# One tile of squares for the norms of a four layer network, and their sum one step later

## Chip, cores and metric
The kernel runs on one core of a Trainium2 chip. The metric is the device time of one execution in microseconds, as the median of several runs. TensorE multiplies, ScalarE applies functions and casts, VectorE and GpSimd do elementwise work, SyncE issues the DMAs.

## What is computed
Two layers of one block, then two of another, on 256 tokens of 1024 features in float32. Every layer normalises its input twice. Cut to what matters here:

```python
def rms_norm(x, w):
    y = x * lax.rsqrt(jnp.mean(x * x, axis=-1, keepdims=True) + 1e-6) * w
for l in range(2):                       # layers 0 and 1
    h = rms_norm(x, mix_pre_norm[l]);  m = hybrid_mixer(h, w_in[l], ...)
    x = x + rms_norm(m, mix_post_norm[l])
    h = rms_norm(x, ffn_pre_norm[l])
    x = x + rms_norm((silu(h @ w_gate) * (h @ w_up)) @ w_down, ffn_post_norm[l])
for l in range(2):                       # layers 2 and 3
    h = h + hybrid_mixer_2(rmsnorm(h, attn_norm[l]), w_in[l], ...)
    h = h + square(relu(rmsnorm(h, mlp_norm[l]) @ w_up[l])) @ w_down[l]
return rmsnorm(h, final_norm)
```
The eight norms ahead of a projection are those of the change. The first projection of a mixer is `qkv` (with a convolution of four taps along time and a Silu behind it), of an attention `q2a`, of an ffn `gu`, of an mlp `up`.

## The kernel before
Activations are kept turned: features on the 128 partitions, 256 tokens along the row, eight tiles `xT`. Weights stream in blocks of 128 x 1024 (`raw`, four slots), block after block over the whole network. ScalarE casts each to its high half (`whi`), VectorE, for some blocks (`SHARED`) GpSimd, subtracts it to get the low half (`wlo`, four slots). A product of float32 is three products: high weights with high and low activations, low weights with high activations; a block has 24 of them. In the mixers' `qkv` blocks 4, 8 and 12 of the layer are GpSimd's.

A norm is taken after the projection. The input is only scaled by its gain and split (`hh`, `hl`), the projection runs on that, and a factor per token, `RSB` = exp(-0.5 ln(mean + eps)), is multiplied in when a pair of result tiles is read out of its bank. The sum over features is made with a matrix of ones: ScalarE squares four pairs of tiles (`SQ2`, 128 x 512 each), GpSimd adds pair 0 to pair 1 and pair 2 to pair 3 (`squares`), TensorE multiplies the four halves with ones into one bank (`norm_sum`), ScalarE takes Ln and Exp (`factor`), VectorE turns the factor for the norms in `BY_TOKEN`.

Every engine runs its own queue in the order of the program. Each walks a projection in steps (`Job.steps`): step 0 has blocks 0 and 1, then one block a step; every second step completes a pair of tiles, which is read out (`evac`: VectorE multiplies by `RSB`; in `qkv` ScalarE then makes the first tap and VectorE three more for each tile). At each step ScalarE and VectorE first split the blocks of `STAGED`, which are two to four blocks ahead: at step 0 blocks 2 and 3, at step 1 blocks 4 and 5. The `hook` is the norm's part: on TensorE `norm_sum` behind step 0, on ScalarE and VectorE the factor behind the splits of step 0, ahead of the first pair. In a mixer, `next(qkv)` twice, then the small products of the gates (`SW`, 16 and 8 columns), then `delta(L)`, whose first part is a chain of tiny instructions with Exp and Ln between VectorE and ScalarE. ScalarE holds one table of functions at a time; Exp and Ln share one, Silu has another.

Of the kernel before, what the change touches and what calls it, by code (L numbers as in the profile page):

```python
# [15 lines left out]
T = 256  # L16
# [248 lines left out]
def program(nc, ins, out):  # L265
    with ExitStack() as ctx:
# [338 lines left out]
        def scalar(a):  # L605
# [20 lines left out]
            def project(name, L, evac=None, hook=None):  # L626
                for chunks, done in JOBS[name, L].steps():
# [3 lines left out]
                    if hook and len(chunks) == 2:  # L631
                        hook()
                    for m0 in done:
                        if evac:
                            a.wait_ge(*proj.at(name, L, m0))
                            evac(m0)
# [189 lines left out]
            def first(L):  # L826
# [30 lines left out]
                next(qkv)  # L857
                a.wait_ge(*v_dn.at("ab", L))
# [195 lines left out]
        def vector(v):  # L1054
# [14 lines left out]
            def project(name, L, evac=None, hook=None):  # L1069
                for chunks, done in JOBS[name, L].steps():  # L1070
# [3 lines left out]
                    if hook and len(chunks) == 2:  # L1074
                        hook()
                    for m0 in done:
                        if evac:
                            evac(m0)
# [236 lines left out]
            def first(L):  # L1315
# [20 lines left out]
                qkv = project("qkv", L, conv, hook)  # L1336
                next(qkv)
# [315 lines left out]
        def gpsimd(g):  # L1653
# [18 lines left out]
            def squares(norm, j):  # L1672
                if j % 2:
                    g.wait_ge(*a_norm.at("square", norm, j))
                    tt(pair(SQ2, j), pair(SQ2, j), pair(SQ2, j - 1), OP.add).then_inc(*g_norm.up("squares", norm, j))

            def all_squares(then):
                for j in range(4):
                    squares(then, j)
# [88 lines left out]
            def first(L):  # L1768
                qkv = project("qkv", L)
                next(qkv)  # L1770
                next(qkv)
                dn = delta(L)
# [68 lines left out]
            for j in range(4):  # L1841
                squares("mixpre0", j)
# [9 lines left out]
        def tensor(e):  # L1852
# [30 lines left out]
            def project(name, L, xh, xl, ready, hook=None, after=None):  # L1883
                job = JOBS[name, L]
                for chunks, done in job.steps():
                    if len(chunks) == 2:
# [11 lines left out]
                        if hook:  # L1898
                            hook()
                    else:  # L1900
                        i = chunks[0]
                        e.wait_ge(*wlo_at(i))
                        for q in range(8):
# [11 lines left out]
                            elif full:  # L1915
                                x.then_inc(*proj.up(*full))
                    if after:
# [97 lines left out]
            def norm_sum(norm):  # L2015
# [3 lines left out]
                for j in (1, 3):  # L2019
                    e.wait_ge(*g_norm.at("squares", norm, j))  # L2020
                    for k in range(2):
                        x = mm(bank[b][:, 0:T], C("ones"), pair(SQ2, j)[:, k * T:(k + 1) * T], (j, k) == (1, 0), (j, k) == (3, 1))
                x.then_inc(*e_norm.up("sum", norm))
# [194 lines left out]
            def first(L):  # L2218
                norm = f"mixpre{L}"
                h = hh, hl, stream_ready(norm)  # L2220
                qkv = project("qkv", L, *h, lambda: norm_sum(norm))
                next(qkv)
# [352 lines left out]
```

## Time and profile before

| | |
|---|---|
| median of 3 runs | 1928.36 us (1928.3 to 1932.68) |
| profiled execution, its own time | 1935.99 us |
| its span | 1934.2 us |
| TensorE busy | 1887.0 us, 98% |
| VectorE busy | 1238.2 us, 64% |
| ScalarE busy | 958.4 us, 50% |
| GpSimd busy | 311.4 us, 16% |
| chain that ended last | PE 83%, DVE 12%, ACT 4% |

The profile names the engines PE (TensorE), DVE (VectorE), ACT (ScalarE), POOL (GpSimd) and SP (SyncE). A row of the timeline has the start and the length in us, the engine, the line, the operation, what is written and read with their shapes, how many in a row, and in brackets the idle time of the engine before it with what ended it. A float32 product with ones is two rows' worth, so four of them are x8. Products overlap their neighbours: the distance of two starts is what one costs.

### The profile page before, as it was taken

The numbers are of one execution on the slowest core, as the hardware profiler recorded it, in microseconds if no ns is written. First come the engines' busy times: TensorE is split into PE (matmuls) and PEld (weight loads), VectorE is DVE, ScalarE is ACT, GpSimd is POOL, SyncE is SP. The second block draws the span as 40 slices with busy tenths as digits, with TensorE's granted clock in tenths as the row PEclk, the third lists the DMA queues.
The fourth block names the chain that finished last, engine by engine and source line by source line (L and its number), as shares of the span: only waits on it lengthen the run. The fifth ranks groups of instructions, "written<-read, shape, count | busy, mean of one in ns | idle before, by whom it ended". The sixth has DMA issues, their size and how long they took to land.

```text
span 1934.2 us, 35101 instructions
## 1 busy us (share of the span) xinstructions
PE 1887.0 (98%) x14820; PEld 1800.6 (93%) x14820; DVE 1238.2 (64%) x1667; ACT 958.4 (50%) x1375; POOL 311.4 (16%) x174
## 2 busy tenths in 40 slices
PE   7999999999999999999999999999999999999998
PEld 7989998998889999999988999999999999999997
DVE  6884577665579545867657775577646684567743
ACT  5533365544563344654445445655534444656632
POOL 1050121000014102200001352310000353220000
PEclk9999999999999999999999999999999999999999
DMA  5443344656344323545665553345555763345652
GB/s 209 158 138 108 121 161 140 215 196 205 134 142 159 115 99 127 201 164 186 196 206 176 178 190 121 132 153 198 188 186 172 219 191 123 131 161 176 197 196 99
DMA packets 91580, 317.50 MB, mean 164 GB/s; under 512 B 11552, under 2 KB 12704, under 8 KB 91040
## 3 DMA queue, kind: packets, MB, share of 16 engines
q1 hardware_dynamic: 91424, 315.26, 48.7%
q8 instruction: 118, 1.93, 0.4%
q14 instruction: 38, 0.31, 0.0%
HBM read 304.99 MB, written 1.05 MB: 158 GB/s over the span
## 4 chain that ended last, share of the span: by engine, by line
PE 83%; DVE 12%; ACT 4%; issue 1%; DMA 0%; SPq 0%; ACTq 0%; DVEq 0%
PE bank L1863 81%; DVE wlo L1056 4%; DVE area L1056 3%; DVE area L1062 2%; ACT area L618 1%; ACT whi L624 1%; PE bank L2302 1%; PE bank L2042 1%; DVE xT L1062 0%; DMA raw<-in_weights 0%; DVE hl L1062 0%; DVE area L1527 0%; ACT hh L618 0%; DVE area L1525 0%; PE bank L2320 0%
## 5 line engine op out<-in xcount | busy, mean ns | idle before, releaser
L1056 DVE TENSOR_TENSOR wlo<-raw,whi 128x1024 fp32r<-128x1024 f32 x512 | 657.0, 1296 | 427.6 <-ACT whi L624 427.2
L1863 PE MATMUL bank<-hh,whi 128*128 128x256 f32 x2928 | 834.0, 285 | 26.4 <-DVE wlo L1056 18.7
L1863 PE MATMUL bank<-hl,whi 128*128 128x256 f32 x2928 | 817.6, 279 | 0.0
L1863 PE MATMUL bank<-hh,wlo 128*128 128x256 f32 x2928 | 817.4, 279 | 0.0
L624 ACT CAST whi<-raw 128x1024 fp32r<-128x1024 f32 x572 | 588.2, 1046 | 398.5 <-PE bank L1863 368.5
L1863 PEld LDWEIGHTS bank<-hh,whi 128*128 128x128 f32 x2928 | 556.9, 190 | 41.8 <-issue 15.1
L1863 PEld LDWEIGHTS bank<-hl,whi 128*128 128x128 f32 x2928 | 556.0, 190 | 1.5 <-issue 1.4
L1863 PEld LDWEIGHTS bank<-hh,wlo 128*128 128x128 f32 x2928 | 555.7, 190 | 0.0
L1655 POOL TENSOR_TENSOR area<-area 128x512 f32<-128x512 f32 (+4 forms) x90 | 138.3, 1544 | 929.8 <-ACT area L618 675.9
L1655 POOL TENSOR_TENSOR wlo<-raw,whi 128x1024 fp32r<-128x1024 f32 x60 | 151.5, 2526 | 332.1 <-ACT whi L624 331.7
L1863 PE MATMUL bank<-area 128*128 128x128 f32 (+5 forms) x1544 | 200.3, 289 | 4.1 <-DVE area L1056 3.3
L1863 PEld LDWEIGHTS bank<-area 128*128 128x128 f32 (+2 forms) x1544 | 181.2, 188 | 18.4 <-DVE area L1056 4.6
L1863 PE MATMUL bank<-FH,whi 128*128 128x256 f32 x640 | 178.6, 279 | 0.0
L1863 PE MATMUL bank<-FL,whi 128*128 128x256 f32 x640 | 178.3, 279 | 0.0
L1863 PE MATMUL bank<-FH,wlo 128*128 128x256 f32 x640 | 178.2, 279 | 0.0
L618 ACT ACTIVATE area<-area 128x256 f32<-128x256 f32 (+9 forms) x247 | 140.0, 578 | 60.3 <-DVE area L1056 20.7
L1056 DVE TENSOR_TENSOR area<-bank,area 128x512 f32<-128x512 f32 (+4 forms) x194 | 116.6, 629 | 57.1 <-PE bank L1863 52.9
L1863 PEld LDWEIGHTS bank<-FH,whi 128*128 128x128 f32 x640 | 121.5, 190 | 0.1
L1863 PEld LDWEIGHTS bank<-FL,whi 128*128 128x128 f32 x640 | 120.1, 188 | 0.1
L1863 PEld LDWEIGHTS bank<-FH,wlo 128*128 128x128 f32 x640 | 120.1, 188 | 0.0
L1056 DVE TENSOR_TENSOR area<-bank,RSB 128x512 f32<-128x512 f32 (+1 forms) x118 | 80.4, 682 | 51.4 <-PE bank L1863 51.4
L1863 PE MATMUL bank<-wlo,FH 128*128 128x512 f32 x240 | 94.6, 394 | 0.0
(123 smaller groups left out, 1883.6 us busy)
## 6 DMA issues: line engine op xcount, KB each, us to landing
raw<-in_weights SPq DMA_DIRECT2D x572, 512.0 KB, 3.7
area<-area SPq DMA_DIRECT2D x96, 64.0 KB, 3.7
area<-area SPq DMA_DIRECT2D x16, 128.0 KB, 3.8
cst<-in_const SPq DMA_DIRECT2D x1, 1188.0 KB, 10.1
cst<-in_const SPq DMA_DIRECT2D x1, 1024.5 KB, 5.6
xT<-in_x SPq DMA_DIRECT2D x4, 256.0 KB, 5.8
out<-xT SPq DMA_DIRECT2D x1, 1024.0 KB, 3.8
area<-in_lev SPq DMA_DIRECT2D x2, 384.0 KB, 7.7
```

What stands on the lines that cost most here:

```text
L618: return a.activation(dst, src, fn, scale=scale, **more)
L624: a.copy(whi[:, i % RING, :], raw[:, i % RAW, :]).then_inc(*hi.up(i))
L1056: return v.tensor_tensor(dst, x, y, op)
L1062: return v.scalar_tensor_tensor(out=dst, in0=x, scalar=s, in1=y, op0=op0, op1=op1)
L1655: return g.tensor_tensor(dst, x, y, op)
L1863: return e.matmul(ps, x, y, start=start, stop=stop, skip_group_check=skip)
L2042: x = e.transpose(bank[b0 + j][:, 128 * (b % 4):128 * (b % 4) + 128], block(src, b), C("eye"))
L2302: o = e.transpose(bank[b][:, 128 * u:128 * u + 128], x.grid()[:, j % 2, j // 2, 128 * kb:128 * kb + 128], C("eye"))
```

## The change
GpSimd adds the squares up further: the two sums of pairs to one, and its two halves to one tile of 128 x 256. TensorE multiplies that one tile with ones. The hook stands behind step 1 in place of step 0, on all three engines, and the first pair of tiles is read out behind it. In the mixers the part behind the second `next(qkv)` now stands behind a third. VectorE's `project` is changed as ScalarE's, and its, GpSimd's and TensorE's `next(qkv)` too.

```diff
@@ ScalarE
             def project(name, L, evac=None, hook=None):
-                for chunks, done in JOBS[name, L].steps():
+                first_pair = []
+                for step, (chunks, done) in enumerate(JOBS[name, L].steps()):
                     for i in chunks:
                         for s in STAGED[i]:
                             split(s)
-                    if hook and len(chunks) == 2:
+                    if hook and step == 0:
+                        first_pair, done = done, []
+                    if hook and step == 1:
                         hook()
+                        done = first_pair + done
                     for m0 in done:
...
                 qkv = project("qkv", L, conv, hook)
+                next(qkv)
                 next(qkv)
                 next(qkv)
...
@@ GpSimd
-            def squares(norm, j):
-                if j % 2:
-                    g.wait_ge(*a_norm.at("square", norm, j))
-                    tt(pair(SQ2, j), pair(SQ2, j), pair(SQ2, j - 1), OP.add).then_inc(*g_norm.up("squares", norm, j))
-
             def all_squares(then):
-                for j in range(4):
-                    squares(then, j)
+
+                for j in (1, 3):
+                    g.wait_ge(*a_norm.at("square", then, j))
+                    tt(pair(SQ2, j), pair(SQ2, j), pair(SQ2, j - 1), OP.add).then_inc(*g_norm.up())
+                g.wait_ge(*g_norm.now())
+                tt(pair(SQ2, 3), pair(SQ2, 3), pair(SQ2, 1), OP.add).then_inc(*g_norm.up())
+                g.wait_ge(*g_norm.now())
+                tt(SQ2[:, 1536:1536 + T], SQ2[:, 1536:1536 + T], SQ2[:, 1536 + T:2048], OP.add).then_inc(*g_norm.up("squares", then))
...
@@ TensorE
-                        if hook:
-                            hook()
                     else:
...
+                    if hook and step == 1:
+                        hook()
                     if after:
...
                 fresh(b, a_norm.at("log", norm))
-                for j in (1, 3):
-                    e.wait_ge(*g_norm.at("squares", norm, j))
-                    for k in range(2):
-                        x = mm(bank[b][:, 0:T], C("ones"), pair(SQ2, j)[:, k * T:(k + 1) * T], (j, k) == (1, 0), (j, k) == (3, 1))
-                x.then_inc(*e_norm.up("sum", norm))
+                e.wait_ge(*g_norm.at("squares", norm))
+                mm(bank[b][:, 0:T], C("ones"), SQ2[:, 1536:1536 + T], True, True).then_inc(*e_norm.up("sum", norm))
```

TensorE, start of layer 0 (block 1's last products, the ones, block 2; `bank0` is the norm's). Before:

```order
L1863 MATMUL bank4<-hl_58,whi_51 128x256
L1863 MATMUL bank4<-hh_57,wlo_52 128x256
L1863 MATMUL bank0<-area_61,cst_53 128x256 [waits norm_pool]
L1863 MATMUL bank0<-area_61,cst_53 128x256
L1863 MATMUL bank0<-area_61,cst_53 128x256 [waits norm_pool]
L1863 MATMUL bank0<-area_61,cst_53 128x256
L1863 MATMUL bank5<-hh_57,whi_51 128x256 [waits wlo_dve]
L1863 MATMUL bank5<-hl_58,whi_51 128x256
L1863 MATMUL bank5<-hh_57,wlo_52 128x256
```

Now:

```order
L1874 MATMUL bank4<-hl_58,whi_51 128x256
L1874 MATMUL bank4<-hh_57,wlo_52 128x256
L1874 MATMUL bank5<-hh_57,whi_51 128x256 [waits wlo_dve]
L1874 MATMUL bank5<-hl_58,whi_51 128x256
...
L1874 MATMUL bank5<-hl_58,whi_51 128x256
L1874 MATMUL bank5<-hh_57,wlo_52 128x256
L1874 MATMUL bank0<-area_61,cst_53 128x256 [waits norm_pool]
L1874 MATMUL bank5<-hh_57,whi_51 128x256 [waits wlo_dve]
L1874 MATMUL bank5<-hl_58,whi_51 128x256
```

The four products with ones stood between blocks 1 and 2; one stands between blocks 2 and 3.

ScalarE, first projection of layer 0, from the factor on (`RSB` from `bank0` is its Ln, `CAST whi` a high half, 128x8 the gates' chain, 128x512 a Silu and the squares behind it). Before:

```order
L618 ACTIVATE RSB_59<-bank0,cst_53 128x256 [waits norm_pe]
...
L624 CAST whi_51<-raw_50 128x1024 [waits proj,raw0]
L624 CAST whi_51<-raw_50 128x1024 [waits proj,raw1]
L618 ACTIVATE area_61<-area_61 128x8 [waits delta_dve] x2
L618 ACTIVATE area_61<-area_61,cst_53 128x8 [waits delta_act]
L618 ACTIVATE area_61<-par_54 128x8
L624 CAST whi_51<-raw_50 128x1024 [waits proj,raw2]
L618 ACTIVATE area_61<-area_61,par_54 128x256 [waits evac_dve,proj]
L618 ACTIVATE area_61<-area_61,par_54 128x256
L618 ACT_TABLE_LOAD
```

Now, from the two high halves that stand ahead of the factor:

```order
L624 CAST whi_51<-raw_50 128x1024 [waits proj,raw0]
L624 CAST whi_51<-raw_50 128x1024 [waits proj,raw1]
L618 ACTIVATE RSB_59<-bank0,cst_53 128x256 [waits norm_pe]
...
L624 CAST whi_51<-raw_50 128x1024 [waits proj,raw2]
L618 ACTIVATE area_61<-area_61,par_54 128x256 [waits evac_dve,proj]
L618 ACTIVATE area_61<-area_61,par_54 128x256
L618 ACT_TABLE_LOAD
L618 ACTIVATE area_61<-area_61 128x512 [waits delta_dve]
L618 ACTIVATE area_61<-area_61 128x512 [waits delta_act]
L611 ACT_TABLE_LOAD [waits delta_dve]
L618 ACTIVATE area_61<-area_61 128x8
L618 ACTIVATE area_61<-area_61 128x8 [waits delta_dve]
```

The high halves of blocks 4 and 5 have moved ahead of the factor, the second pair's tap and the first pair's Silu ahead of the gates' chain, and two table loads have come in, one ahead of that chain's first Exp and one, below these rows, ahead of the next Silu.

GpSimd, start of layer 0 (`area` 128x512 and 128x256 are the squares, `wlo` are low halves of blocks 4, 8 and 12). Before:

```order
L1655 TENSOR_TENSOR area_61<-area_61 128x512 [waits norm_act] x2
L1655 TENSOR_TENSOR wlo_52<-raw_50,whi_51 128x1024 [waits whi,ldhead]
L1655 TENSOR_TENSOR wlo_52<-raw_50,whi_51 128x1024 [waits whi] x2
L1655 TENSOR_TENSOR area_61<-area_61 128x1024 [waits delta_dve,delta_pe,ldc1]
L1709 COPY area_61<-area_61 128x1024 [waits evac_dve]
```

Now:

```order
L1665 TENSOR_TENSOR area_61<-area_61 128x512 [waits norm_act] x2
L1665 TENSOR_TENSOR area_61<-area_61 128x512 [waits norm_pool]
L1665 TENSOR_TENSOR area_61<-area_61 128x256 [waits norm_pool]
L1665 TENSOR_TENSOR wlo_52<-raw_50,whi_51 128x1024 [waits whi,ldhead]
L1665 TENSOR_TENSOR wlo_52<-raw_50,whi_51 128x1024 [waits whi] x2
```

Two adds stand between the squares and the low half of block 4, each behind a wait for the one before.

## Rows read from the trace of the kernel before

**Rows 1.** Page, costliest groups, TensorE (busy, mean ns; idle before, releaser):
```profile
L1863 PE MATMUL bank<-hh,whi 128*128 128x256 f32 x2928 | 834.0, 285 | 26.4 <-DVE wlo L1056 18.7
```

**Rows 2.** Timeline, TensorE, mixer 0 (start, length, what, times; idle before):
```profile
19.22 1.89 PE L1863 MATMUL bank<-area,cst 128*128 128x256 f32 x8
21.06 0.28 PE L1863 MATMUL bank<-hl,whi 128*128 128x256 f32 x1
```

**Rows 3.** Timeline, TensorE, attention 2, the key's norm:
```profile
1059.18 0.59 PE L1863 MATMUL bank<-area,cst 128*128 128x256 f32 x2
```

**Rows 4.** Timeline, GpSimd, TensorE and VectorE, ffn of layer 0:
```profile
332.83 2.53 POOL L1655 TENSOR_TENSOR area<-area 128x512 f32<-128x512 f32 x2 [30.89 <-ACT area L618]
...
334.46 2.09 PE L1863 MATMUL bank<-area,cst 128*128 128x256 f32 x8
...
334.77 1.68 DVE L1056 TENSOR_TENSOR wlo<-raw,whi 128x1024 fp32r<-128x1024 f32 x1 [2.15 <-ACT whi L624]
...
336.51 0.38 PE L1863 MATMUL bank<-hh,whi 128*128 128x256 f32 x1
...
339.33 0.28 PE L1863 MATMUL bank<-hh,whi 128*128 128x256 f32 x1
...
342.29 0.38 PE L1863 MATMUL bank<-hh,whi 128*128 128x256 f32 x1
```

**Rows 5.** Timeline, mixer of layer 1, then attention of layer 2:
```profile
521.66 2.53 POOL L1655 TENSOR_TENSOR area<-area 128x512 f32<-128x512 f32 x2 [186.30 <-ACT area L618]
...
525.33 0.38 PE L1863 MATMUL bank<-hh,whi 128*128 128x256 f32 x1
...
1032.91 1.60 DVE L1056 TENSOR_TENSOR wlo<-raw,whi 128x1024 fp32r<-128x1024 f32 x1 [2.21 <-ACT whi L624]
...
1034.57 0.38 PE L1863 MATMUL bank<-hh,whi 128*128 128x256 f32 x1
```

**Rows 6.** Timeline, VectorE and TensorE, mlp of layer 2:
```profile
1297.98 1.72 DVE L1056 TENSOR_TENSOR wlo<-raw,whi 128x1024 fp32r<-128x1024 f32 x1 [0.52 <-ACT whi L624]
...
1299.74 1.89 PE L1863 MATMUL bank<-area,cst 128*128 128x256 f32 x8
...
1307.58 0.38 PE L1863 MATMUL bank<-hh,whi 128*128 128x256 f32 x1 [0.50 <-DVE wlo L1056]
```

**Rows 7.** Timeline, GpSimd and VectorE where they meet, mixer 0:
```profile
25.81 2.35 POOL L1655 TENSOR_TENSOR wlo<-raw,whi 128x1024 fp32r<-128x1024 f32 x1 [10.76 <-ACT whi L624]
...
121.12 2.39 POOL L1655 TENSOR_TENSOR area<-area 128x1024 f32<-128x1024 f32 x1
...
121.39 3.20 DVE L1056 TENSOR_TENSOR wlo<-raw,whi 128x1024 fp32r<-128x1024 f32 x1 [1.67 <-ACT whi L624]
...
123.46 2.29 POOL L1655 TENSOR_TENSOR area<-area 128x512 f32<-128x512 f32 x1
```

**Rows 8.** Timeline, VectorE, mixer 0, first projection:
```profile
22.10 0.43 DVE L1056 TENSOR_TENSOR area<-RSB,cst 128x256 f32<-128x256 f32 x1 [4.83 <-ACT RSB L618]
24.36 5.12 DVE L1062 SCALAR_TENSOR_TENSOR area<-area,par 128x255 f32<-128x255 f32 x6 [0.64 <-ACT area L618]
...
33.97 1.23 DVE L1056 TENSOR_TENSOR wlo<-raw,whi 128x1024 fp32r<-128x1024 f32 x1 [0.67 <-ACT whi L624]
36.43 2.96 DVE L1062 SCALAR_TENSOR_TENSOR area<-area,par 128x255 f32<-128x255 f32 x6 [0.64 <-ACT area L618]
40.39 1.22 DVE L1056 TENSOR_TENSOR wlo<-raw,whi 128x1024 fp32r<-128x1024 f32 x1 [0.99 <-ACT whi L624]
```

**Rows 9.** Timeline, ScalarE, same stretch:
```profile
36.82 1.28 ACT L618 ACT_TABLE_LOAD   x1
38.11 1.30 ACT L618 ACTIVATE area<-area 128x512 f32<-128x512 f32 x2
```

**Rows 10.** Timeline, TensorE, later in mixers 0 and 1:
```profile
54.28 0.39 PE L1863 MATMUL bank<-hh,whi 128*128 128x256 f32 x1 [0.73 <-DVE wlo L1056]
...
545.86 0.39 PE L1863 MATMUL bank<-hh,whi 128*128 128x256 f32 x1 [1.43 <-DVE wlo L1056]
```

More of the change, by code:

```diff
@@ L1069, in project @@
             def project(name, L, evac=None, hook=None):
-                for chunks, done in JOBS[name, L].steps():
+                first_pair = []
+                for step, (chunks, done) in enumerate(JOBS[name, L].steps()):
                     for i in chunks:
@@ L1073, in project @@
                             split(s)
-                    if hook and len(chunks) == 2:
+                    if hook and step == 0:
+                        first_pair, done = done, []
+                    if hook and step == 1:
                         hook()
+                        done = first_pair + done
                     for m0 in done:
@@ L1336, in first @@
                 qkv = project("qkv", L, conv, hook)
+                next(qkv)
                 next(qkv)
@@ L1771, in first @@
                 next(qkv)
+                next(qkv)
                 dn = delta(L)
@@ L1839, in second @@
                     all_squares("attn3")
-            for j in range(4):
-                squares("mixpre0", j)
+            all_squares("mixpre0")
             g.wait_ge(s_head, 16)
@@ L1884, in project @@
                 job = JOBS[name, L]
-                for chunks, done in job.steps():
+                for step, (chunks, done) in enumerate(job.steps()):
                     if len(chunks) == 2:
@@ L1916, in project @@
                                 x.then_inc(*proj.up(*full))
+                    if hook and step == 1:
+                        hook()
                     if after:
@@ L2221, in first @@
                 qkv = project("qkv", L, *h, lambda: norm_sum(norm))
+                next(qkv)
                 next(qkv)
```

## The prediction

> **What bounds the kernel now.** I read the page's groups first: TensorE is busy almost all the time, and its idle time in front of the first product of a weight block is 26.4 us over 2928 products, of which 18.7 us end with a low half (wlo) from VectorE [rows 1]. So a microsecond of products taken away shortens the run only where the next block's low half is ready; elsewhere it turns into idle time. I therefore went to each of the eight places with the timeline, all engines side by side, and asked there what releases the first product of the third weight block. I call the blocks of a projection 0, 1, 2, ... and their low halves wlo(0), wlo(1), ...
>
> **What the sum costs TensorE.** In layer 0 the four products with ones are eight passes; from their start to the second product of block 2 it is 21.06 - 19.22 = 1.84 us [rows 2]. A product of 256 columns takes (339.33 - 336.51) / 24 = 0.12 us [rows 4], so the four cost 1.72 us, 0.43 each. The one kind of place with a single such product agrees: its two passes take 0.59 us where the eight take 1.89 [rows 2, 3], and (1.89 - 0.59) / 3 is 0.43. Three removed at eight places are at most 8 x 1.29 = 10.3 us. That is the ceiling of this part, and 0.53% of the time.
>
> **Where that is hidden already.** In the ffn of layer 0 step 0 ends at 334.46, the sum fills 334.46 to 336.51, and block 2 starts at 336.51. But wlo(2) ran from 334.77 for 1.68 us, so until 336.45; block 2 starts 0.06 us after it [rows 4]. TensorE could not have begun block 2 earlier. The sum lies in a wait that is there anyway. With the change TensorE idles from 334.58 to 336.5, starts block 2 at the same time, and then pays for the one product, 0.43, plus about 0.15 for the restart after waits. Before, block 4 began at 342.29, 0.13 later than two blocks of 2.83 after 336.51 would give; that bit goes. The place becomes 0.45 slower (the sum of ffn 1 shows the same times from its start). The attention of layer 2 is alike: wlo(2) ends at 1034.51, block 2 starts at 1034.57 [rows 5]. Its block 4 had no such bit to lose, so it gets 0.6 slower. In the mixer of layer 1 the squares end at 524.19 and block 2 starts at 525.33 [rows 5], in the same order of events; its account is below.
>
> At the two mlp and in the attention of layer 3 the squares come earlier. In the first mlp wlo(2) ends at 1299.70, when step 0 does, at 1299.74 [rows 6]. Block 2 can follow at once, three products (1.29) are saved, and the wait of 0.50 for wlo(4) in front of block 4 [rows 6] goes too, because ScalarE now splits blocks 4 and 5 ahead of its wait for the sum. Less a restart and a short wait for GpSimd (0.3): -1.5 at each mlp, -1.1 in the attention of layer 3, which has no such wait.
>
> **The two new adds on GpSimd.** Two adds of 512 columns take 2.53 us together [rows 4], so the third takes 1.27 and the one of 256 columns, by half, 0.64. They meet VectorE. A VectorE instruction of two SBUF operands doesn't run beside one of GpSimd: a low half that started at 121.39 inside a GpSimd instruction that ended at 123.51 took 3.20 us instead of 1.22, and GpSimd's next one, begun at 123.46, took 2.29 instead of 1.27: it stood until VectorE was done at 124.59 [rows 7]. The two take turns. So the third add waits for wlo(2) and runs to 337.6, wlo(3) then ends at 338.7, the fourth add at 339.3. TensorE wants the sum at 339.33. It fits with nothing to spare, hence the 0.1 to 0.2 us per place above; if VectorE won the turn once more it would be 1.1 us at each of seven places.
>
> **The mixers' first projection.** Here VectorE is the bound: TensorE waits 0.73 for it at 54.28 in layer 0, and 1.43 at 545.86 in layer 1 [rows 10]. So it is VectorE's chain from the factor on that counts, up to wlo(7), at 40.39 in layer 0 [rows 8]. Step by step, layer 0:
> factor: the sum starts 2.83 us later (a block) and is three products shorter (1.29): +1.54;
> the six taps of the first pair took 5.12 us, those of the second 2.96, because GpSimd's wlo(4), at 25.81 for 2.35, stood against them [rows 7, 8]; wlo(4) is now made ahead of the factor, in VectorE's idle time: -2.16;
> wlo(5) too, which stood in the chain: -1.2 (its 1.22, overlapped by 0.08);
> the third step now lies ahead of the gates' small chain and holds the second pair, with its Silu. The small chain needs Exp and Ln again. The order above shows three table loads where there was one; the load takes 1.28 [rows 9]. The one ahead of the first Exp lies in VectorE's path: +1.28. The second Silu load sits beside the taps of the third pair: +0.2;
> VectorE's waits for high halves (0.67 ahead of 33.97, 0.99 ahead of 40.39 [rows 8]) become one of 0.7: -1.0.
> Sum -1.3 us for layer 0.
> The Trainium skill (ScalarE: Activation LUTs, "What ACT_TABLE_LOAD costs") puts a switch of tables at about 2.7 us with its drain. The trace differs: the load at 36.82 takes 1.28, and the function behind it starts at 38.11, with no drain to be seen [rows 9]. By the page's figure the loads would cost 2.8 us more over both layers and the sum would turn to +1.4 us.
>
> Layer 1 differs in one thing: the first two adds end only at 524.19 [rows 5], so the four fill GpSimd to about 528.2, and wlo(4) is done behind them and behind VectorE's wlo(5), from 529.2 to 531.5. The factor's product on VectorE is due at 529.8 and has two SBUF operands: it stands until 531.5. The chain starts 5.1 us late instead of 1.5. Sum +2.4 us. Without that collision it is +0.8; and TensorE idles for about 1 us ahead of the gates' products and 3.5 us ahead of block 7.
>
> **Other queues.** SyncE waits for low halves only, and those of blocks 4 and 5 come earlier. The swaps of the rope wait for products that come 1 to 3 us later; the fetch behind the first of them waits for wlo(6), which stands behind that product on VectorE anyway: nothing. The factor reads the norm's bank at once after the sum, and a projection wants that bank back two blocks later at the earliest: no wait.
>
> **Sum.** -1.3 (mixer 0) + 2.4 (mixer 1) + 0.9 (two ffn) + 0.6 (attention 2) - 3.0 (two mlp) - 1.1 (attention 3) = -1.5 us. The profiled execution took 1935.99 us, its span 1934.2; the median of the runs is 1928.36. I take the difference over as it is: 1934.5 for a profiled execution, 1927 for the median.
>
> **Rivals.**
> 1. The products were the cost, as a count of TensorE's work would have it: the low halves come earlier too, because ScalarE and VectorE no longer stand at the factor. Then the 10.3 us come, and the waits of 0.5 at the two mlp: 1918. Against it: wlo(2) depends on nothing that the change moves, and it gates four of the eight places. A half-way form, mixers gaining 2.5 each, gives 1922. Together 0.13; about 0.11 of it beyond 0.3%.
> 2. Slower: the place is VectorE's chain in the mixers' projection. Its order against GpSimd shifts, and the two later halves that GpSimd makes in each layer, wlo(8) and wlo(12), fall wholly on taps, as wlo(4) did at 2.16. That is a bound, since a part of it is paid now: four times 2.16 is 8.6 us, and the sum ends at 1935.6. It decides from 7.3 us lost in both layers together, which is the 0.3% and my gain of 1.5. For it: the shift of 1.5 and 5.1 us is certain, and a tap that meets a half has always waited for the whole of it. Against it: VectorE's chain sets when both are made, so they move together. Chance 0.14.
> 3. GpSimd wins the ports ahead of wlo(2), or VectorE wins them once more ahead of the fourth add: 1.1 to 1.3 us (one add, or one low half) at seven places, 1935. Against it the row of 123.46 [rows 7], and the semaphore between the adds. Chance 0.08.
> 4. The change moves what it says, but later waits for VectorE swallow or return it: within 2 us of 1928. This is part of the forecast's range.
> 5. A table load costs more in the path than its 1.28 us, at most twice that: two in each layer make 2.6 to 5.1 us, 1930 to 1932. Against it the row of 38.11 [rows 9]. Chance 0.03, inside the forecast's range; this is what the page's figure would do.
>
> **How the numbers follow.** Forecast 0.65, its own range 1923 to 1932; rival 1 0.13, 2 and 3 0.22. About 0.3% (5.8 us) is what a measurement of this kernel tells from no change. Faster than that: 0.13 (rival 1 and a tail of the forecast). Slower: 0.18 (most of 2 and 3). Same: 0.69. The range 1921 to 1935.5 holds the forecast, the half-way form of rival 1 and the near half of 2 and 3.
>
> **What the new profile would show.** In both ffn and in attention 2: idle TensorE of about 1.9 us ahead of block 2, ended by a low half, block 2 at the same distance from step 0 as before. In both mlp: no wait ahead of block 2, none ahead of block 4. On ScalarE three table loads in each mixer's first projection. In layer 1 a factor's product of about 2 us on VectorE, under a GpSimd instruction, and a wait of TensorE of about 3 us ahead of block 7. The prediction is wrong if wlo(2) starts earlier than now, if the third add delays it, or if the waits in the mixers differ from this by more than 2 us.

## The result, and the profile after

The changed kernel took 1941.15 us (median of 11 runs, 1935.41 to 1950.37), the kernel before 1932.68 (11 runs, 1926.9 to 1938.17): ratio 1.0046, 95% interval 1.003 to 1.0061. It is slower, and the forecast of 1927.0 with 0.69 on "same" was wrong. The forecast started from the 1928.36 of three runs of the kernel before; from the 1932.68 of eleven its -1.5 us would be 1931.2, and the measured difference is +8.5. The profiled execution of the changed kernel took 1940.96 us, 4.97 more than that of before.

Page of the changed kernel, TensorE's first group, the one of [rows 1]:

```profile
L1874 PE MATMUL bank<-hh,whi 128*128 128x256 f32 x2928 | 840.3, 287 | 32.2 <-DVE wlo L1061 24.5
```

The idle time ahead of these products rose by 5.8 us, all of it ended by low halves. But the mean product also became 2 ns longer (287, before 285), though the array does the same. The forecast had no term for that. I laid the 12,720 products with high and low halves of both traces side by side, one by one, and read how far the second is behind at the start of each block. "So far" adds up:

| place | forecast | measured | so far |
|---|---|---|---|
| mixer 0 | -1.3 | -1.3 | -1.3 |
| between, clock | | +1.6 | +0.3 |
| ffn 0, up to block 4 | +0.45 | +1.9 | +2.3 |
| ffn 0, the rest of `gu` | 0 | +4.1 | +6.4 |
| mixer 1 | +2.4 | +2.2 | +8.6 |
| between, clock | | -1.5 | +7.1 |
| ffn 1, up to block 4 | +0.45 | +2.0 | +9.1 |
| ffn 1, the rest of `gu` | 0 | +3.1 | +12.2 |
| attention 2 | +0.6 | +2.1 to +2.4 | +14.6 |
| between, pace and clock | | +0.6 | +15.2 |
| mlp 2, up to block 4 | -1.5 | -1.4 | +13.8 |
| mlp 2, the rest of `up`, and `down` | 0 | -6.4 | +7.4 |
| attention 3 | -1.1 | -0.9 | +6.5 |
| between | | +0.2 | +6.7 |
| mlp 3 | -1.5 | -1.7 | +5.0 |

Timeline of the changed kernel, in order of time: ScalarE in mixer 0; ffn 0, from its block 0 on; GpSimd and VectorE in mixer 1; the sum of mlp 2.

```profile
31.65 1.28 ACT L618 ACT_TABLE_LOAD   x1
...
34.75 1.28 ACT L611 ACT_TABLE_LOAD   x1 [0.51 <-DVE area L1061]
...
41.70 1.28 ACT L618 ACT_TABLE_LOAD   x1
...
328.89 0.35 PE L1874 MATMUL bank<-hh,whi 128*128 128x256 f32 x1 [1.58 <-DVE hl L1067]
...
333.17 6.44 POOL L1665 TENSOR_TENSOR area<-area 128x512 f32<-128x512 f32 x4 [30.87 <-ACT area L618]
...
335.11 6.72 DVE L1061 TENSOR_TENSOR wlo<-raw,whi 128x1024 fp32r<-128x1024 f32 x4 [2.14 <-ACT whi L624]
...
336.84 0.38 PE L1874 MATMUL bank<-hh,whi 128*128 128x256 f32 x1 [1.88 <-DVE wlo L1061]
...
338.00 0.42 PE L1874 MATMUL bank<-hh,wlo 128*128 128x256 f32 x1
...
341.29 0.59 PE L1874 MATMUL bank<-area,cst 128*128 128x256 f32 x2
...
528.07 6.43 POOL L1665 TENSOR_TENSOR area<-area 128x512 f32<-128x512 f32 x4 [188.46 <-ACT area L618]
534.47 3.37 POOL L1665 TENSOR_TENSOR wlo<-raw,whi 128x1024 fp32r<-128x1024 f32 x1
...
537.79 0.43 DVE L1061 TENSOR_TENSOR area<-RSB,cst 128x256 f32<-128x256 f32 x1 [2.20 <-ACT RSB L618]
...
1318.10 0.67 PE L1874 MATMUL bank<-area,cst 128*128 128x256 f32 x2
```

In ffn 0 the order of events is the forecast one, up to block 2: TensorE idles 1.88 us and starts when the low half is there, and the four adds end at 339.61 (forecast 339.3). But where [rows 4] have 2.83 us for a block, block 2 now takes 341.29 - 336.84 = 4.45: its products last 0.42 from 337.7 on. TensorE by stretch says why (length, busy time with the number of products, then PEclk, the granted clock: 1.00 is 2.4 GHz, 0.50 is 1.2 GHz; then the DMA's share and GB/s). The changed kernel:

```profile
334.80:336.80 2.00, 0.17 (x2) 1.00 0.00 0
337.70:341.10 3.40, 3.40 (x18) 0.50 0.74 242
342.00:345.00 3.00, 3.00 (x27) 1.00 0.81 264
849.70:853.10 3.40, 3.40 (x18) 0.50 0.62 193
1047.70:1051.00 3.30, 3.30 (x18) 0.50 0.75 223
...
345.00:449.00 104.00, 104.00 (x885) 1.00 0.59 193
...
1320.00:1465.00 145.00, 145.00 (x1282) 1.00 0.62 200
```

The three rows at 0.50 stand right behind the idle time of ffn 0, ffn 1 and attention 2. Each costs about 1.6 us, and the trace of before has none in these places. This is the first missing term.

The second: behind block 4 the clock is full again, and still the changed kernel falls back, evenly, by 0.1 us a block. The last two rows show it as a number of products, in `gu` of layer 0 and from `up` of layer 2 into the `down` that follows it without a wait. The same two stretches of the kernel before, run a second time:

```profile
345.00:449.00 104.00, 104.00 (x920) 1.00 0.62 205
...
1320.00:1465.00 145.00, 145.00 (x1233) 1.00 0.58 187
```

In 104 us at full clock TensorE starts 885 products in the one and 920 in the other: 117.5 and 113.0 ns each. In `up` it is the other way round. By the distances of single starts there are two values only in these stretches, 113.3 and 117.8 ns, and a stretch keeps its value until TensorE waits or runs a product of another kind (a foreign product, such as the one with ones). I call them the fast and the slow pace, and name a stretch by the projection that it starts in. The Trainium skill (TensorE: Matmul & The Clock Gate, "Wait — 56ns, not 53.3ns?") gives a product at full clock its columns by 2.4 GHz and 2.5 ns more, for 256 columns an estimate of 109 ns; the trace has neither that nor a single value.

At the mlp the forecast held: block 2 and block 4 wait no more than 0.04 us, where [rows 6] had 0.50, and the one product stands behind block 2. ScalarE's table loads in mixer 0 stand where the order had them, 1.28 us each as in [rows 9]. In mixer 1 the size was right (+2.2) and the way was not: the factor's product on VectorE was to stand under GpSimd's low half for about 2 us. It takes 0.43, because half clock at 532 had made the sum so late that GpSimd was done, at 537.84. Nor is there a wait of 3 us ahead of block 7.

### The profile page after: what moved, and what is told of

Same layout as the page of the kernel before. It is cut to its first block, busy times and chain, and to the rows that moved or that the text cites. A ratio compares the mean times of both kernels' runs of the same rounds, so it can differ in the third digit from the quotient of the medians.

```text
span 1939.2 us, 35025 instructions
## 1 busy us (share of the span) xinstructions
PE 1886.2 (97%) x14772; PEld 1802.5 (93%) x14772; DVE 1247.7 (64%) x1667; ACT 964.0 (50%) x1379; POOL 338.7 (17%) x190
## 4 chain that ended last, share of the span: by engine, by line
PE 85%; DVE 10%; ACT 4%; issue 1%; DMA 0%; SPq 0%; DVEq 0%; ACTq 0%
PE bank L1874 83%; DVE wlo L1061 4%; DVE area L1061 3%; ACT area L618 2%; ACT whi L624 1%; DVE area L1067 1%; PE bank L2311 1%; DVE xT L1067 1%; PE bank L2050 1%; ACT hh L618 0%; DVE hl L1067 0%; DMA raw<-in_weights 0%; PE bank L2329 0%; DVE area L1119 0%; ACT L618 0%
## 5 line engine op out<-in xcount | busy, mean ns | idle before, releaser
L1061 DVE TENSOR_TENSOR wlo<-raw,whi 128x1024 fp32r<-128x1024 f32 x512 | 665.9, 1315 | 427.0 <-ACT whi L624 426.5
L1874 PEld LDWEIGHTS bank<-hh,wlo 128*128 128x128 f32 x2928 | 561.9, 192 | 0.0
L1665 POOL TENSOR_TENSOR area<-area 128x512 f32<-128x512 f32 (+4 forms) x106 | 165.7, 1570 | 919.8 <-ACT area L618 666.8
L1874 PE MATMUL bank<-whi,FL 128*128 128x512 f32 x240 | 94.4, 393 | 0.0
```

Source lines behind the costliest of these rows:

```text
L1061: return v.tensor_tensor(dst, x, y, op)
L1665: return g.tensor_tensor(dst, x, y, op)
L1874: return e.matmul(ps, x, y, start=start, stop=stop, skip_group_check=skip)
```

## The experiments

Two theories went into the first runs. A: what TensorE idles at four places costs more than the time it idles, by the clock and the pace behind it. B: VectorE's chain in the mixers' first projections costs it (my rival 2). The first expectation alone calls something else theory B: that the pace comes out by chance in each execution.

**The kernel before, again**, to see what a trace varies by itself.

> The kernel before, unchanged, as a control: how much of the difference between two executions is not the change. Theory A (the extra time of the change comes from what the idle time at the four places does to TensorE's clock): ratio 1.000, and no half-clock window behind the first products of an ffn, an mlp or an attention, as in the first profile. Theory B (the pace of the products, 113 or 118 ns, is chance from execution to execution, and the two profiles differ by such luck): the profile shows the slow pace in other stretches than the first one (there: layer 2's mlp, 1308 to 1480 us), and its length can differ by up to 6 us.

Measured: 1933.26 against 1932.36 us, ratio 1.0002 [0.999, 1.0015]. No half clock stands at the places of the ffn, mlp and attentions, and the slow pace is in `up` of layer 2 again, as in the first trace.

**The tile alone, the hook in its old place.**

```diff
@@ the kernel before
-                for j in (1, 3):
-                    e.wait_ge(*g_norm.at("squares", norm, j))
-                    ... four products
+                ... and the four adds on GpSimd, as in the change
+                e.wait_ge(*g_norm.at("squares", norm))
+                mm(bank[b][:, 0:T], C("ones"), SQ2[:, 1536:1536 + T], True, True).then_inc(*e_norm.up("sum", norm))
```

> Only the first part of the change: the squares added up to one tile, one product with ones, at the old place behind step 0. By my account of GpSimd's adds (the third waits for wlo(2), the fourth for wlo(3)) TensorE waits for the tile: at ffn 0 the tile is there at 339.3 where step 0 ends at 334.5, so 3.2 us slower than before at each of the two ffn, the attention of layer 2 and the mixer of layer 1 there hidden in part; about 1.8 slower at each mlp and attention 3; mixer 0 1.3 faster. Sum +12 us, ratio 1.006, more if the waits lower the clock (1.009). If the adds are not held up by VectorE (rival), the tile is there 2.0 us after the pairs and the sum is +4 us, ratio 1.002.

Measured: 1960.45 us, ratio 1.0147 [1.0116, 1.0178]. TensorE stands in front of the one product until GpSimd's adds end:

```profile
338.06 1.19 PE L1863 MATMUL bank<-area,cst 128*128 128x256 f32 x2 [4.75 <-POOL area L1655]
```

Four places idle 4.7 us, as the expectation's times give for ffn 0 (339.3 less 334.5), and three more 2.7 to 2.9; each of the first four has half clock at the end of its idle time or right behind it, and so have two of the three. The loss is above the expected 1.006 to 1.009; in the trace 11.9 of its 25.2 us are half clock (table below), and the rest is near the expected 12. Here the adds themselves are late; the step's delay is what hides them.

**The step alone, four products and two adds as before.**

```diff
@@ the changed kernel
-                mm(bank[b][:, 0:T], C("ones"), SQ2[:, 1536:1536 + T], True, True).then_inc(*e_norm.up("sum", norm))
+                for j in (1, 3):
+                    ... the four products and their waits, and GpSimd's two adds
```

> Only the second part: the hook one step later, the first pair behind it, a third step ahead of the gates in the mixers; the squares stay two tiles of 512 columns and TensorE keeps four products with ones. Against the changed kernel it has three products more at eight places (1.29 each, 10.3 us if all show, 6 to 8 where VectorE doesn't hide them) and less GpSimd work. Theory A: the four waits of 1.9 us stay and the clock windows behind them too, so it is 6 to 8 us slower than the changed kernel, ratio 1.008. Rival (the two adds on GpSimd cost the time by standing against VectorE): the loss goes with them and the ratio is 1.003 or less.

Measured: 1959.88 us, ratio 1.0138 [1.0117, 1.016], above the 1.008. The waits were as expected (1.87 us in the row below, 1.80 to 1.88 at the other places). The clock was not: of the three places of ffn and attention 2 only ffn 1 has half clock behind it (the row at 0.50). All the long stretches ran at the slow pace, which the expectation had no term for:

```profile
335.58 0.39 PE L1873 MATMUL bank<-hh,whi 128*128 128x256 f32 x1 [1.87 <-DVE wlo L1061]
...
335.60:338.90 3.30, 3.30 (x26) 1.00 0.67 209
850.70:854.10 3.40, 3.40 (x19) 0.50 0.77 241
1049.10:1052.50 3.40, 3.38 (x27) 1.00 0.68 189
...
345.00:449.00 104.00, 104.00 (x885) 1.00 0.59 194
...
1320.00:1465.00 145.00, 145.00 (x1227) 1.00 0.59 191
```

**The changed kernel with the idle time filled** at both ffn, mixer 1 and attention 2, by products whose result is thrown away.

```diff
@@ the changed kernel, TensorE, behind step 0
+            def filler(norm):
+                if norm in FILLED:
+                    b = NORM_BANK[norm]
+                    fresh(b, a_norm.at("log", norm))
+                    for _ in range(4):
+                        mm(bank[b][:, 0:T], C("ones"), cst[:, 0:T], True, True)
```

> The changed kernel with four products of ones with constants (result thrown away) behind step 0 of the two ffn, mixer 1 and attention 2, where TensorE waits 1.8 to 1.9 us for wlo(2): the wait is filled with work and nothing else changes. Theory A: block 2 starts when it did, no half-clock window follows, and block 2 takes 2.8 instead of 4.3 us: 1.5 us less at three places, about 4.5 us less than the changed kernel, ratio to before 1.002. Rival (the clock's windows come by chance or with the gates' small products): windows stay, time as the changed kernel, 1.0046.

Measured: 1935.6 us, ratio 1.0012 [0.9999, 1.0024]. Four products a place that compute nothing took away some 0.3% of the time; the two intervals do not meet. At the places TensorE ran at full clock throughout, and `gu` of layer 0 fast:

```profile
337.60:341.00 3.40, 3.40 (x27) 1.00 0.52 161
846.00:849.40 3.40, 3.40 (x28) 1.00 0.55 177
1039.90:1043.30 3.40, 3.40 (x27) 1.00 0.51 159
```

**The change by places.** In the next three the new scheme stands only where `LATE` says; the other places are those of the kernel before.

```diff
+ONE_TILE = ("ffnpre0", "ffnpre1", "attn2")
+LATE = (("gu", 0), ("gu", 1), ("q2a", 2))
@@ ScalarE and VectorE
+                    late = (name, L) in LATE
+                    if hook and late and step == 0:
+                        first_pair, done = done, []
+                    if hook and step == (1 if late else 0):
                         hook()
+                        done = first_pair + done
```

> The new scheme (one tile, sum and factor a step later) only in the two ffn and in the attention of layer 2, where TensorE now idles 1.9 us ahead of block 2; the other five places as before. Theory A (the idle time lowers the clock behind it, and the restart leaves the long stretch of products at 118 ns each in place of 113): 1.9 + 1.9 + 2.1 for the places and up to 8.4 for the pace behind them, ratio 1.003 to 1.0075. Rival B (the loss is in VectorE's chain of the mixers' first projections): 1.9 by my forecast's three terms or less, ratio 1.001.

Measured: 1941.75 against 1933.59 us, ratio 1.0038 [1.001, 1.0067]. That lies in the lower half of theory A's range, and the interval reaches down to rival B's 1.001. In its trace only the middle place has half clock behind it, and the other two then cost 0.3 and 0.9 us, which is what the forecast had for them (0.45 and 0.6):

```profile
336.10:339.40 3.30, 3.30 (x28) 1.00 0.62 184
840.70:844.00 3.30, 3.30 (x17) 0.50 0.72 216
1035.70:1039.00 3.30, 3.30 (x28) 1.00 0.68 180
```

The mixers alone (`LATE` has both `qkv`):

> The new scheme only in the two mixers, with the third step ahead of the gates. Theory A: -1.3 in layer 0 and +2.2 in layer 1, ratio 1.0005, between 0.9995 and 1.0015. Rival B: the whole loss is here, ratio 1.004 or more.

Measured: 1934.73 us, ratio 0.9997 [0.9977, 1.0018]: theory B falls. Layer 0 gives -1.3 and layer 1 +2.2 again, and here, with the sum in time, the collision of the forecast is seen, 1.81 us for a product of 0.43:

```profile
530.13 1.81 DVE L1065 TENSOR_TENSOR area<-RSB,cst 128x256 f32<-128x256 f32 x1 [0.73 <-ACT RSB L620]
```

The four places with early squares (mixer 0, both mlp, attention 3):

> The new scheme only at the four places where the squares come early and the forecast gave a gain: mixer of layer 0, both mlp, attention of layer 3. By the aligned traces -1.3 - 1.4 - 0.9 - 1.7 = -5.3 us, ratio 0.9973. If the long up projection of layer 2 also runs at 113 ns a product in place of 118, 6.4 less still: 0.994. Rival C (pace and clock come out by chance wherever the program is changed, the sums of the places do not add up): ratio 1.000 or above.

Measured: 1927.51 us, ratio 0.9957 [0.9939, 0.9976]. Faster than both kernels. Its trace is of the fastest of the eleven runs, 1922.86. The same kernel once more:

> The kernel with the new scheme at four places once more, for a second interval and a second trace. Ratio 0.9957 to 0.9973; no wait ahead of block 2 in either mlp, none ahead of their block 4, no stretch at half clock behind these places. If its gain over the 5.3 us of the places came from the pace, the trace shows which long stretches run at 113 ns.

Measured: 1931.26 against 1932.62 us, ratio 0.9987 [0.9966, 1.0007]. The gain is smaller and its interval touches none; the two intervals overlap by little. In the first trace every long stretch was fast, in the second the `up` of layer 3 was slow, 6 us of the 11.4 between the two traces.

**The changed kernel again.**

> The changed kernel again, unchanged, for a second trace: ratio 1.0046, between 1.003 and 1.006. Theory A has the waits of 1.9 us in the same places, most of them with a stretch at half clock behind. If the pace of products belongs to the program, both gu and the attention of layer 2 run at 118 ns again and both up at 113; if it is drawn anew in each run, other stretches do.

Measured: 1938.98 us, ratio 1.0025 [1, 1.005]. The three stretches at half clock are there again (337.0, 845.6 and 1040.2), but the slow pace sits elsewhere: `gu` of layer 0 is fast, `up` of layer 3 slow:

```profile
345.00:449.00 104.00, 104.00 (x920) 1.00 0.60 195
...
1770.00:1915.00 145.00, 145.00 (x1233) 1.00 0.58 184
```

The first stretch of `gu` of layer 1 and attention 2 are slow again and `up` of layer 2 is fast again. So the pace of a stretch can differ between two executions of one program; whether some stretches are slow more often than others, two traces can't tell.

**Filler at the three places alone, and less idle time without a move.**

> The kernel with the new scheme in the two ffn and the attention of layer 2, with four products of ones with a constant (their result is thrown away) put where the old four stood, at these three places. TensorE is then busy where it idled, and block 2 starts no later. Theory A (idle time costs by the clock and pace behind it): the stretches at half clock and the long stretches at 118 ns behind these places go; left are 0.45, 0.45 and 0.6 to 0.9 of the one product, ratio 1.001, against 1.0038 without the filler. Rival (the new order on ScalarE and VectorE costs it): ratio stays at 1.003 or more.

Measured: 1938.32 against 1932.62 us, ratio 1.0024 [1.0002, 1.0045], without the filler 1.0038: undecided. The half clocks are gone, but in its trace, of one of the slower runs (1943.7), both `up` were slow.

In the next one only the last of the four products with ones is left at four places:

```diff
@@ the kernel before, TensorE, at both ffn, mixer 1 and attention 2
                     for k in range(2):
+                        if norm in LESS and (j, k) != (3, 1):
+                            continue
...
```

> The kernel before with only the last of the four products with ones at both ffn, the mixer of layer 1 and the attention of layer 2, nothing moved. It leaves three quarters of those norms' sums out. By my forecast's count block 2 waits for its low half anyway, so nothing changes: ratio 1.000. Theory A: TensorE idles about 0.9 us in place of 1.29 us of products ahead of block 2, or up to 1.9 if it starts the product late; if this lowers the clock or the pace behind, +1.5 to +4 at each place, ratio 1.003 to 1.006. Between them lies a threshold in the idle time.

Measured: 1931.7 us, ratio 0.9983 [0.9963, 1.0003]. TensorE idles 0.8 to 0.9 us at the four places, 0.3 more ahead of block 2, and no half clock follows right behind at any, so 0.9 us did not cost what theory A had for it:

```profile
335.32 0.67 PE L1864 MATMUL bank<-area,cst 128*128 128x256 f32 x2 [0.89 <-POOL area L1656]
```

**Can the pace be held?** A small product (ones, 8 columns, overwritten) was put into the long stretches, first at every fourth pair.

```diff
@@ TensorE, project, at the start of a pair of tiles
                                 fresh(b, leaves(name, L, m0))
+                                if name in ("gu", "up") and m0 % 8 == 0:
+                                    mm(bank[b][:, 0:8], C("ones"), cst[:, 0:8], True, True)
```

> The kernel before with one product of ones with 8 columns of a constant (overwritten) ahead of every fourth pair of tiles in the gu and up projections, 26 in all. If a foreign product redraws the pace of the products behind it, the trace shows both 113 and 118 ns inside one long stretch, changing at these products alone, where before each stretch holds one; the mean of the time is about that of before plus 26 x 0.15 = 4 us, 1.002, and its spread over runs is smaller. Rival: the pace is set by waits alone, and a stretch keeps its pace across them.

The expectation's 26 is a wrong count: the trace has 16 of them, because the branch of blocks 0 and 1 has none, and by 0.15 us each that is 2.4 us, ratio 1.0012.

Measured: 1933.16 us, ratio 0.9998 [0.9981, 1.0015], with all 12 runs within 4.8 us (before: 17.5 in 35 runs, more runs and so a wider range by itself). `up` of layer 2 starts slow, at 117.8 ns; behind the small product at 1322.82 and its first neighbours it stands at 113 and stays there to its end:

```profile
1322.70 0.28 PE L1863 MATMUL bank<-hh,wlo 128*128 128x256 f32 x1
1322.82 0.28 PE L1863 MATMUL bank<-cst 128*128 128x8 f32 x2
1322.96 0.36 PE L1863 MATMUL bank<-hh,whi 128*128 128x256 f32 x1
...
1323.51 0.28 PE L1863 MATMUL bank<-hl,whi 128*128 128x256 f32 x1
1323.63 0.28 PE L1863 MATMUL bank<-hh,wlo 128*128 128x256 f32 x1
1323.74 0.28 PE L1863 MATMUL bank<-hh,whi 128*128 128x256 f32 x1
1323.85 0.28 PE L1863 MATMUL bank<-hl,whi 128*128 128x256 f32 x1
```

`up` of layer 3 does the same at its first small product, at 1768.42, and fast stretches stay fast: the rival, that waits alone set the pace, falls. So the same small product was put at block 4 of `gu`, `q2a` and `up` (`m0 == 4`), into four kernels:

> The kernel before with one product of ones with 8 columns of a constant (overwritten) at the start of block 4 of each gu, q2a and up projection, six in all. Theory (the pace of a long stretch is drawn by the last wait or foreign product ahead of it, and this small product always gives 113 ns): the up of layer 2, at 118 ns in most traces of this order, runs at 113: -6.4 us in most runs, + 6 x 0.23 for the products. Ratio 0.9975, and a spread of half that of before. Rival: the small product only happened to stand in fast stretches: ratio 1.000 and the same spread.

Measured: 1942.83 against 1936.92 us, ratio 1.0032 [1.0014, 1.0049], where 0.9975 was expected: the theory of the held pace falls. In the kernel before, block 4 of both `up` waits, and there the small product stands right behind a wait. Both `up` then ran slow behind it:

```profile
1312.28 0.39 PE L1863 MATMUL bank<-cst 128*128 128x8 f32 x2 [0.30 <-DVE wlo L1056]
```

> The changed kernel with the same six small products. If the pace carried most of its loss (both gu, the attention of layer 2, the up of layer 3 at 118 ns in one or both traces: 8 us on average): ratio to before 0.9995 to 1.0005. What is left against before_held, 2.8 us by the aligned traces (mixers -1.3 and +2.2, ffn and attention 2 with the half clock 1.9 + 1.9 + 2.1, mlp and attention 3 -4.0), makes 1.0015 to it. If the clock carried it and not the pace: ratio to before stays 1.003 or more.

Measured: 1936.64 us, ratio 1.0002 [0.9984, 1.002]. The changed kernel doesn't wait at block 4, and with the small product the loss is gone: the interval of the first comparison, 1.003 to 1.0061, lies wholly above it, that of the second overlaps. How much of that is the pace isn't shown. The trace is of the fastest of the 12 runs (1928.34): in it all long stretches but `gu` of layer 1 were fast, but attention 2 also had no half clock behind its idle time of 1.80 us.

```profile
345.00:449.00 104.00, 104.00 (x920) 1.00 0.61 196
1320.00:1465.00 145.00, 145.00 (x1282) 1.00 0.63 198
```

> The kernel with the new scheme in the two ffn and the attention of layer 2 alone, with the six small products. The pace is held at 113 ns, left are the three places, with 1.5 us more each where a stretch at half clock follows: 0.3 + 0.5 + 0.9 without, 1.9 + 1.9 + 2.1 with. Against before_held +1.7 to +5.9 us, against before ratio 0.9985 to 1.0005. Without small products it was 1.0038.

Measured: 1946.25 us, ratio 1.0048 [1.0026, 1.007], where 1.0005 at most was expected; both `up` slow, as in before_held. The pace wasn't held here. Against before_held it is +3.4 us, inside the expected 1.7 to 5.9.

> The kernel with the new scheme at the four places with early squares, with the six small products. Its places give -5.3 us and the pace is held: ratio to before 0.995, to before_held 0.997, spread small. If it isn't below before_held by more than 3 us, the gain of the four places was pace and not products.

Measured: 1930.99 us, ratio 0.9965 [0.995, 0.9981]; both `gu` slow (their block 4 waits, 0.05 to 0.07 us), both `up` fast. It is 0.6% under before_held, but since the pace wasn't held in either, that is no measure of the products.

**What all traces say together.** At the last product with halves each trace is some time behind the first one of before. I split that into: idle time ahead of TensorE's instructions (gaps over 15 ns); half of the time at half clock; slow pace (4.5 ns for each of its products, in `gu`, `up` with the `down` behind it, and attention 2's `q2a`). The rest should be the products taken out, 1.29 us a place:

| kernel | behind | idle | clock | pace | rest | products |
|---|---|---|---|---|---|---|
| before, again | -2.7 | -1.7 | -1.7 | +0.4 | +0.3 | 0 |
| changed | +5.0 | +5.7 | +8.5 | +2.8 | -12.1 | -10.3 |
| changed, again | +5.3 | +6.3 | +6.8 | +2.2 | -10.1 | -10.3 |
| changed, small product | -7.6 | +7.3 | 0 | -4.6 | -10.4 | -10.3 |
| changed, filled | -4.4 | +1.2 | +1.7 | -6.4 | -1.0 | -3.4 |
| ffn and attention 2 alone | +2.7 | +4.1 | 0 | +2.3 | -3.8 | -3.9 |
| mixers alone | -2.6 | +2.5 | 0 | -6.0 | +0.9 | -2.6 |
| four places | -13.1 | -1.1 | -1.7 | -6.3 | -4.1 | -5.2 |
| four places, again | -1.7 | 0 | +1.7 | +0.8 | -4.3 | -5.2 |
| tile alone | +25.2 | +25.3 | +11.9 | -1.3 | -10.8 | -10.3 |
| step alone | +24.4 | +4.8 | +3.4 | +15.7 | +0.4 | 0 |
| less of the sum | +3.1 | +3.1 | +3.4 | +0.2 | -3.7 | -5.2 |
| before, every fourth pair | +0.6 | +0.6 | 0 | -4.2 | +4.2 | 0 |
| before, small product | +11.4 | -0.5 | -1.7 | +10.2 | +3.4 | 0 |
| ffn and attention 2, filled | +7.7 | -0.7 | 0 | +8.4 | 0 | +1.3 |
| ffn and attention 2, small product | +8.0 | +8.0 | -3.4 | +6.8 | -3.4 | -3.9 |
| four places, small product | -4.2 | -2.5 | 0 | +1.9 | -3.6 | -5.2 |

(The fillers are counted with the products; the small products and the pace of short stretches are in the rest. It agrees within 3.5 us, but for the small products of the fourth pairs, 4.2.) Of 10.3 us of products the changed kernel gave back 5.7 to 6.3 in idle time (the forecast's -1.5 has 8.8 in it) and 6.8 to 8.5 to the clock, which it had not. Of the clock's part 5.1 us stand behind the idle time of the three places, 1.7 each, and the other 1.7 to 3.4 in mixer 1. In both traces of the changed kernel this alone makes it slower, by 2 to 3 us, and the pace comes on top. In the trace with the small product it does not: two of the three places have half clock there, but elsewhere that trace has less of it than the first one of before.

## Why the prediction was wrong

**What held.** TensorE's cost of the sum; the place by place view of what releases block 2; the four adds on GpSimd, to 0.3 us; mixer 0 (-1.3); both mlp and attention 3 (-4.0, forecast -4.1); ScalarE's table loads; mixer 1 by size. Rival 1 (the whole 10.3 us) and rival 2 (VectorE's chain) are both refuted, the second by the mixers alone, at 0.9997; so is rival 3, since the adds end at 339.61 and not a turn later. Mixer 1 was a right sum by luck in the changed kernel: the collision that was to make it is not in its trace, and half clock took its place. The collision is in the trace of the mixers alone, but the wait of 3.5 us ahead of block 7 isn't there either (0.14). One sum of the forecast is wrong without bearing on the result: rival 1 with mixers gaining 2.5 each adds up to 1920.8, not 1922, just below the stated range.

**The step that failed** is "With the change TensorE idles from 334.58 to 336.5, starts block 2 at the same time, and then pays for the one product, 0.43, plus about 0.15". All of it happened, and it isn't the whole price. I took work out of a wait and held that to be free. In six traces TensorE idles 1.8 to 1.9 us ahead of block 2 of both ffn and of attention 2, and 11 of these 18 places have half clock right behind it (step alone: one of three); in eleven traces without that idle time (one with 0.9 us), 0 of 33, the two filled kernels among them. Where it didn't come the places cost what the forecast had (the step alone, with its four products, apart). Shorter idle time did nothing of the kind: at the same places and in mixer 1 TensorE idles 1.58 us ahead of block 0 (above at 328.89), and in 18 traces no half clock follows there, 0 of 72. The 1.8 us of the change come about 8 us after it. No run tells whether the longer time or the second idle time so soon makes the difference.

**The pace** was the second thing without a term, and the larger one for a single run. What stands last ahead of a stretch bears on it in some cases. Counted over 18 traces, for streams of 20 or more products: behind a wait of under 0.1 us the stream was fast in 32 of 33; behind the small product in a running stream in 31 of 33, but in 1 of 7 where it stood behind a wait. The others are closer to the share of all streams, 60%: behind a wait of 0.1 to 0.9 us 92 of 146, behind a longer one 45 of 59, behind the single product of the sum, met without a wait, 30 of 55. These counts pool the same few places over many traces, so they show no rule of the wait's length alone. Before, `gu` starts its long stretch behind the short wait of [rows 4] at 342.29, and in seven traces of that order both `gu` were fast, 14 of 14. The change puts the product of the sum there: of the first long stretches in `gu` in the traces of the changed kernel and of its ffn alone, 4 of 6 were slow. In `up` of layer 2 the change does the opposite: the wait of 0.3 to 0.5 of [rows 6] goes, behind which the stretch began slow in 6 of 7 traces, and behind the sum it was fast in all five (kernels with the small product at block 4 not counted; behind the four products of the step alone it was slow). That hides part of the loss in the traces, and is part of why the four places once gained more than their 5.3 us.

**What stays open.** Why the pace has two values, and why a wait's length or a product of 8 columns bears on it, isn't settled; the small product shows that it can be changed, not how. How the 0.25 to 0.46% divides between clock and pace is known for traces (8.5 and 2.8, 6.8 and 2.2 us), not for the runs without one. The half clock vanished in both filled kernels, but the pace moved too, in one trace to the better and in one to the worse, so no run changes the clock alone. Nor is it known why the half clock follows in 11 of 18 cases and not in all.

## What to carry to other kernels

Work inside a wait is not always free to remove: where TensorE would idle for nearly 2 us in its place, price the clock behind it, from rows where the granted clock fell, and as a chance, since it fell in 11 of 18. Split such a change by places before judging it: four of the eight gain (0.9957 and 0.9987 in two comparisons), three lose (1.0038), and the whole loses. A trace is one execution and can be of the fastest: read it with the spread of the runs. And a difference of 4% in the distance of products over a 170 us stretch is 6.5 us; count products per stretch in both traces before explaining a difference of that size by an edit.

## What the runs showed of the hardware

- At full granted clock products of 256 columns stood 113.3 or 117.8 ns apart, for up to 170 us without a change; two stretches switched from slow to fast at a small product (1322.82 and 1768.42).
- Behind TensorE's idle time of 1.8 to 1.9 us, some 8 us after one of 1.58, the granted clock fell to half in 11 of 18 cases; behind the 1.58 us in 0 of 72, behind 0.9 us (four places of one trace) in none, and at 4.7 us (tile alone) in 4 of 4.
- VectorE's product of 0.43 us took 1.81 beside a low half of GpSimd, as the forecast had it for mixer 1.
